# One diagonal product for two directions: the sum of both keys, copied through the identity as a mask

## The reference, cut to what matters

```
def hgrn2_direction(q, i, z, lb, ..., reverse):
    k, lf = forget_terms(z, lb)            # key k = (1 - lb) * sigmoid(-z), lf = log f
    S_t = diag(f_t) S_{t-1} + k_t v_t^T    # v is i
    o_t = S_t^T q_t
...
o_f = direction(q, i, zf, forward);  o_b = direction(q, i, zb, backward)
y = readout(o_f + o_b, g, g_norm, w_out)
```

## Time and profile before

| what | value |
|---|---|
| median of 3 runs | 2517.08 us (2509.78 to 2519.22) |
| the profiled execution, its own time | 2514.89 us |
| its span, first to last instruction | 2513.1 us |
| mean granted TensorE clock | 0.961 of full speed |
| PE busy | 2304.8 us, 92% of the span |
| the 8 steps of the recurrence | about 647 to 1178 us of the span |

### The profile page before, as it was taken

The page is one execution under the profiler, slowest core; times in us unless marked ns, Lnnn a source line. Parts: engine busy times, 40 slices in busy tenths (PEclk is TensorE's granted clock), DMA queues, the critical chain, the costliest instruction groups (busy, mean ns, idle before and its releaser), DMA issues. The chain is left out here.

```text
span 2513.1 us, 27699 instructions
## 1 busy us (share of the span) xinstructions
PE 2304.8 (92%) x11647; PEld 1833.9 (73%) x11647; DVE 1062.4 (42%) x1508; ACT 665.8 (26%) x1013; POOL 836.7 (33%) x393
## 2 busy tenths in 40 slices
PE   6989999789899899999699888999998988999998
PEld 3768886674667676788575576888887767788886
DVE  1122435563266656555887444111115764111113
ACT  2222222214244444463210243110012163100011
POOL 0322010430132323232720033554553335554453
PEclk9999999899899999999899998999999999999999
DMA  9221104142111111112211012232323222223322
GB/s 274 80 86 51 35 27 159 50 133 87 33 34 34 34 34 34 34 51 58 73 51 37 32 51 68 84 98 87 100 93 109 70 99 67 73 95 101 101 91 76
DMA packets 166715, 187.43 MB, mean 75 GB/s; under 512 B 17009, under 2 KB 145345, under 8 KB 166465
## 3 DMA queue, kind: packets, MB, share of 16 engines
q1 hardware_dynamic: 159024, 178.56, 21.9%
q10 hardware_dynamic: 6992, 5.01, 0.8%
q0 software_dynamic: 576, 2.10, 0.2%
HBM read 183.56 MB, written 2.10 MB: 74 GB/s over the span
## 5 line engine op out<-in xcount | busy, mean ns | idle before, releaser
L2793 POOL TENSOR_TENSOR weights_lo<-weights_raw,weights_hi 128x2048 fp32r<-128x2048 f32 (+1 forms) x104 | 470.1, 4520 | 894.3 <-ACT weights_hi L1317 682.4
L641 PE MATMUL ring<-input_hi,weights_hi 128*128 128x512 f32 x784 | 305.4, 390 | 0.0
L642 PE MATMUL ring<-input_lo,weights_hi 128*128 128x512 f32 x784 | 305.0, 389 | 0.0
L643 PE MATMUL ring<-input_hi,weights_lo 128*128 128x512 f32 x784 | 305.0, 389 | 0.0
L2641 DVE CAST weights_hi<-weights_raw 128x2048 fp32r<-128x2048 f32 (+1 forms) x72 | 86.7, 1204 | 378.5 <-PE ring L643 173.9
L2784 POOL TENSOR_TENSOR h_w<-h_p 128x512 f32<-128x512 f32 x56 | 71.2, 1271 | 451.6 <-PE ring L922 367.5
L895 PE MATMUL obank<-acts,weights_raw 128*128 128x512 f32 x384 | 178.1, 619 | 0.8 <-issue 0.8
L642 PEld LDWEIGHTS ring<-input_lo,weights_hi 128*128 128x128 f32 x784 | 147.2, 188 | 30.9 <-issue 0.2
L641 PEld LDWEIGHTS ring<-input_hi,weights_hi 128*128 128x128 f32 x784 | 147.1, 188 | 30.7 <-issue 0.2
L643 PEld LDWEIGHTS ring<-input_hi,weights_lo 128*128 128x128 f32 x784 | 147.1, 188 | 30.6
L906 PE MATMUL obank<-weights_raw,acts 128*128 128x256 f32 x640 | 143.6, 383 | 0.0
(11 more groups left out here) (458 smaller groups left out, 4527.8 us busy)
## 6 DMA issues: line engine op xcount, KB each, us to landing
weights_raw<-in_w_ada SPq DMA_DIRECT2D x24, 1024.0 KB, 5.2
weights_raw<-in_ffn_w_gate SPq DMA_DIRECT2D x22, 1024.0 KB, 5.1
weights_raw<-in_ffn_w_up SPq DMA_DIRECT2D x22, 1024.0 KB, 5.1
weights_raw<-in_w_in_c SPq DMA_DIRECT2D x20, 1024.0 KB, 5.2
weights_raw<-in_ffn_w_down SPq DMA_DIRECT2D x16, 1024.0 KB, 5.0
weights_raw<-in_w_in_ab SPq DMA_DIRECT2D x11, 1024.0 KB, 5.1
weights_raw<-in_w_out_ab SPq DMA_DIRECT2D x8, 1024.0 KB, 5.2
weights_raw<-in_ev_w_in SPq DMA_DIRECT2D x8, 1024.0 KB, 5.7
```

Source lines behind the costliest of these rows:

```text
L641: pe.matmul(o, hi[:, k, ms], xh[:, k, t0:t0 + n], start=k == 0, stop=False)
L642: pe.matmul(o, hi[:, k, ms], xl[:, k, t0:t0 + n], start=False, stop=False)
L643: last = pe.matmul(o, lo[:, k, ms], xh[:, k, t0:t0 + n], start=False, stop=k == KD - 1)
L2793: pool.tensor_tensor(W_LO[slot][:, 0:kt, :], WR[:, slot, 0:kt, :], w_hi[:, 0:kt, :], ALU.subtract).then_inc(sem("w_lo"), 1)
```

## The change

The diagonal product is made once for each pair of heads, in the backward step, with the sum of the keys of both directions. DVE makes that sum (`keys_of_both`) at the end of the forward step, after `state_operands` of the backward step, in place in `HK[0]`. The diagonal is no longer cut out by multiplying with the identity and adding: it is copied over `h_scores` by `copy_predicated`, with the bits of the identity as the mask. PE waits for the sum (semaphore `hg_k_both`) before the diagonal product. ACT waits for that product before it overwrites `HK[0]`.

```
-                pe.wait_ge(sem("hg_k"), st + 1)
                 pe.wait_ge(*product_emptied(("q", hb, 1)))
-                ps = take(f"dg{st}", "v")
-                ...  8 matmuls K_ x Q_
+                if d:
+                    pe.wait_ge(sem("hg_k_both"), hb + 1)
+                    ps = take(f"dg{st}", "v")
+                    ...  8 matmuls HK[0] x Q_
                 pe.wait_ge(sem("hg_ks"), st + 1)
...
             def keys(st):
                 if st >= 2:
                     act.wait_ge(sem("hg_w"), 7 * (st - 1))
+                if st >= 2 and st % 2 == 0:
+                    act.wait_ge(*fill_of(f"dg{st - 1}"))
...
             def diagonal(st):
-                idb = IDENT.unsqueeze(1).to_broadcast([P, TL * HH, P])
-                if d == 0:
-                    dve.tensor_tensor(S[:, :, :], src, idb, ALU.mult).then_inc(emptied["v"], 1)
-                    dve.wait_ge(*read_of(f"dg{st}"))
-                else:
-                    dve.tensor_tensor(HDG[:, :, :], src, idb, ALU.mult).then_inc(emptied["v"], 1)
-                    dve.wait_ge(*read_of(f"dg{st}"))
-                    link(dve.tensor_tensor(S[:, :, :], S[:, :, :], HDG[:, :, :], ALU.add))
+                own = IDENT.bitcast(U32).unsqueeze(1).to_broadcast([P, TL * HH, P])
+                dve.copy_predicated(HSC[STEPS[st][0] % 2][:, :, :], own, src).then_inc(emptied["v"], 1)
+                dve.wait_ge(*read_of(f"dg{st}"))
+
+            def keys_of_both(hb):
+                k0, k1 = HK[0][:, :, 0:L], HK[1][:, :, 0:L]
+                dve.wait_ge(sem("hg_k"), 2 * hb + 2)
+                dve.tensor_tensor(k0, k0, k1, ALU.add).then_inc(sem("hg_k_both"), 1)
...
             for st, (hb, d) in enumerate(STEPS):
                 level_operand(7 * st)
-                diagonal(st)
+                if d:
+                    diagonal(st)
                 level_operand(7 * st + 1)
...
                 level_scores(st, 5)
                 if more:
                     state_operands(st + 1)
-                else:
+                if d == 0:
+                    keys_of_both(hb)
+                if not more:
                     s5_row_columns()
...
                 level_scores(st, 6)
```

More of the change, by code:

```diff
@@ L224, in program @@
         HKT = [view(gt_at + D, 4 * HH, P, name="h_kt"), view(xc + 1280, HH, P, name="h_kt")]
-        HDG = view(bc_at + D, TL * HH, P, name="h_diag")
         HO = view(hi_at, TL, D, name="h_out")
@@ L956, in _ @@
                 b, q = st % 2, hb % 2
-                K_, Q_, I_ = HK[b], HQ[q], HI[q]
+                Q_, I_ = HQ[q], HI[q]
                 seq = hg_seq(d)
@@ L964, in between @@
                         product(slots[i])
-                pe.wait_ge(sem("hg_k"), st + 1)
                 pe.wait_ge(*product_emptied(("q", hb, 1)))
-                ps = take(f"dg{st}", "v")
[L969 to L973, removed]
+                if d:
+                    pe.wait_ge(sem("hg_k_both"), hb + 1)
+                    ps = take(f"dg{st}", "v")
+                    for j in range(TL * HH):
+                        ch, h = divmod(j, HH)
+                        last = pe.matmul(ps[:, j * P:(j + 1) * P], HK[0][:, h, ch * P:(ch + 1) * P],
+                                         Q_[:, h, ch * P:(ch + 1) * P], start=True, stop=True)
+                    last.then_inc(filled, 1)
                 pe.wait_ge(sem("hg_ks"), st + 1)
@@ L2129, in diagonal @@
             def diagonal(st):
-                hb, d = STEPS[st]
                 dve.wait_ge(*fill_of(f"dg{st}"))
                 src = bank(f"dg{st}")[:, :].rearrange("p (j c) -> p j c", j=TL * HH)
-                idb = IDENT.unsqueeze(1).to_broadcast([P, TL * HH, P])
-                S = HSC[hb % 2]
-                if d == 0:
-                    dve.tensor_tensor(S[:, :, :], src, idb, ALU.mult).then_inc(emptied["v"], 1)
-                    dve.wait_ge(*read_of(f"dg{st}"))
-                else:
-                    dve.tensor_tensor(HDG[:, :, :], src, idb, ALU.mult).then_inc(emptied["v"], 1)
-                    dve.wait_ge(*read_of(f"dg{st}"))
-                    link(dve.tensor_tensor(S[:, :, :], S[:, :, :], HDG[:, :, :], ALU.add))
+                own = IDENT.bitcast(U32).unsqueeze(1).to_broadcast([P, TL * HH, P])
[5 more added lines that the diff above has]
+                dve.tensor_tensor(k0, k0, k1, ALU.add).then_inc(sem("hg_k_both"), 1)
             def level_scores(st, i):
```

## The result

The changed kernel takes 2524.6 us (2521.22 to 2529.79, 7 runs) against 2517.08 us: the ratio is 1.0036 (the medians alone give 1.0030), 95% interval 1.0022 to 1.005. It is slower by 0.36%, some 7.5 us by the medians and 9 us by the ratio, less than the 0.5% that the prediction set as its bound. The profiled execution took 2524.0 us, span 2522.2 us, clock 0.956.

The account below looks back on a forecast made before the run. PE was taken as the bound, with DVE mattering only where PE waits at the joints. Terms -4.5 + 6.7 + 1.6 = +3.8 us gave 2518.7 us, stated as 2521 us; own range 2515 to 2523, 8-in-10 range 2511 to 2528.

Parts of the forecast that it names:

- rival B: Joints of steps 1, 3, 5: PE's unbroken rest halves the clock; +6 to +12.6 us, chance 0.13; beyond 12.6 us, 0.06.
- Backward joints, +6.7 us: Steps 1, 3, 5: PE waits for DVE's sum, then diagonal product and copy; level 0 starts 2.23 us later at each.
- upper bound of 10.7: Steps 1, 3, 5: at most 10.7 us lost over the three joints, with the diagonal product at half clock.
- the extra 0.57: Sum on DVE beside POOL's instruction: 0.57 us added to 1.22, giving 1.79 us, from level 6's score copy.
- the disagreement that the prediction saw: Level 6's masked copy, 1.29 us, against the skill's claim that a DVE instruction with one SBUF input is not held.
- step 7: Last backward joint: the sum is ready by 1108.5, before PE arrives at 1110.25, so nothing is lost.
- the middle of full and half clock: Diagonal product in steps 1, 3, 5: level 0 1.37 or 3.09 us later by clock, taken as 2.23 us.
- Forward joints, -4.5 us: Steps 0, 2, 4, 6: without the diagonal product level 0 waits only for its operand, winning 1.13 us at each.
- Behind the joints, +1.6 us: Product after a joint: a longer rest lowers the clock over one more stretch, 1.6 us, not three.
- the removed additions: Four DVE additions of 1.22 us each, before level 1's operand: worth nothing, hidden by a product of 7.08 us.
- ACT's new wait: Middle of the backward step, ACT waiting for the diagonal product behind three products of 7.08 us: costs nothing.
- Rival A: Steps 1, 3, 5: DVE reaches the sum early, so those joints cost nothing; 2512.6 or 2509.8 us, chance 0.16.

Follow-up runs that it names:

- the second ones: Second profiles, nothing altered: the changed kernel again, timed 2523.63 us (ratio 1.0029), and the kernel before again as control, 2523.04 us (ratio 1.0015).

## Why the prediction was right in its range, step by step

*Direction and range: right, with luck in the sum.* 2524.6 us lie within 2511 to 2528, and the change is slower by less than 0.5%. The value of 2521 us was 3.6 too low, about half of the loss, and the measured time lies outside the forecast's own range of 2515 to 2523 us, in the band that rival B had at 0.13. In the first pair of traces the recurrence lost 3.6 us where the sum said 3.8, but that is luck: its terms were off in opposite directions. Measured were about -5.0 us at the four forward joints (-4.5), +10.4 at the three backward ones (+6.7), and -1.8 in place of +1.6 behind the joints.

*Backward joints, +6.7 us: right mechanism, undersized.* They measured +10.4 us in the first profiles (3.48, 3.48, 3.44), near the upper bound of 10.7, and +12.9 us in the second ones, above it. Three terms were off. The sum took 2.06 us, not 1.79: I chose the extra 0.57 from the score copy of level 6, 1.29 against 0.72, and put it down to POOL. That reading was wrong. After the change this copy stands behind POOL's instruction, which ends at 852.27, and still takes 1.28 us; the copies of levels 5 and 6, whose runs are two elements and one, all take 1.28 to 1.33, in every step. So the 1.29 us are no sign of a hold by POOL, and the disagreement that the prediction saw in them falls with the reading. The Trainium skill's rule (SBUF — State Buffer, section "Who interferes with whom") had it better: POOL ends at 852.27, 1.22 us more give 853.49, and the sum ended at 853.35; in steps 1 and 5 it ended 1.1 us after POOL as well. In step 7, with POOL at rest, the sum took 1.21 us. (The rule was written out in the prediction, and not used in its sum.) Second, I took the middle of full and half clock for the diagonal product, and it ran at half clock in all three steps (3.69 to 3.75 us). Third, the score copy behind the sum was counted at 0.72 us and kept its 1.28; at half clock the product hides that, at full clock it would have made DVE, not the product, end the joint. The masked copy's 1.31 us fits the 1.25.

*Forward joints, -4.5 us: the step that failed.* The joints did become 1.2 us shorter, within a tenth of a us of the 1.13 foretold (1.3 in step 0). But the step said that PE's missing work "turns into waiting for the operand" and left it at that. The waiting has a price behind it: PE rested 2.2 to 2.3 us in front of level 0 in place of 1.7, and level 0 and its product ran slower, by 1.7 to 3.4 us where the kernel before had 0 to 1.7. With the useless products put back, 1.2 us shorter joints and full clock came together, and medians lower by 7.5 and 6.1 us with them. In the first pair of traces the 3.7 us won at the joints 2, 4 and 6 stand against 3.4 us more behind them, so this half of the change gave next to nothing.

*Behind the joints, +1.6 us: wrong place.* I counted it behind the backward joints, whose slow stretch in fact moved into the joint (4.2 and 1.7 us less behind steps 3 and 5), and saw none behind the forward ones. Rival B named the right cause, the unbroken rest at the backward joints, and missed the rest at the forward ones. Here the rule of the Trainium skill (TensorE: Matmul & The Clock Gate, section "What's actually happening"), that the slow clock is the resting state and activity releases it, agrees with the traces in kind: with the forward products kept the time behind the forward joints fell from 1.7 to 3.4 us to 0.03 us. All five kernels with useless products also have medians lower by 6 to 10 us, but the filler in the wait for the sum left the product of steps 3 and 5 at half clock, after a rest of 2.3 us.

*Worth nothing, as foretold:* the removed additions, ACT's new wait, step 7 (6.55 us joint against 6.48).

*Rival A fell:* PE waited 6 us for the sum in steps 3 and 5, and 4.3 us in step 1. *What stays open:* the profiles of the recurrence differ by 0.3 to 5.0 us, whichever two of the four are compared, where the timed runs differ by 7 to 9. With single executions of one kernel 10.7 us apart, the remainder cannot be split between a lasting effect outside the joints and chance.

## What to carry to other kernels

Where PE waits for another engine at a joint, taking work off PE gains at most the shorter chain and can cost clock on everything behind it; price both, and try the same edit with the removed work kept as filler, which separates the two in one run. The filler must last up to the work that it is to keep at full clock: in steps 3 and 5 here it ended 2.3 us early and the product behind it stayed slow. Before moving work onto the engine whose chain ends the joint (here DVE, 2.06 us of sum for 1.83 us of PE), count that chain from its first instruction, and look at who else reads the same memory at that moment. When single executions of one kernel differ by more than the effect, compare the same joints in several traces and leave the ratio to many runs.

## What the runs showed that I had not expected

- The kernel before, executed 12 times, fell in two clusters 10 us apart (2512 to 2517 and 2523 to 2526 us), and 35 more executions beside them spread from 2508 to 2526 us. Two traces of it, 10.7 us apart, have the same PE instructions and the same joints within 0.05 us; they differ in where half clock falls.
- Kernels with useless matmuls in PE's waits had lower medians: by 7 us with 48 products of 128 x 128 in the waits for the sum, by 7.5 us with 32 in the four forward joints, by 6 us with 24 more in step 0. For the 32 the traces show where (the time behind the joints); for the other two they show 1.5 us at one joint, and 0.9 us at step 0.
- A masked copy of 128 x 512 from PSUM takes 0.70 to 0.74 us with runs of four elements or more and 1.28 to 1.33 us with runs of one or two, while the diagonal's copy of 128 x 1024, whose runs are whole rows, takes 1.28 to 1.31 us.
